# Split expert down pieces: lower halves computed by GpSimd in two operations, upper halves earlier in ScalarE's order, one-hot tables moved

## The reference

```python
def swiglu(x, w_gu, w_dn):
    g, u = jnp.split(x @ w_gu, 2, axis=-1)
    return (jax.nn.silu(g) * u) @ w_dn

for e in range(N_EXPERTS):
    out = out + comb[..., e:e + 1] * swiglu(x, w_gu[e], w_dn[e])
```

## Time and profile before

| what | value |
|---|---|
| median of 3 runs | 1162.55 us (1162.32 to 1163.24) |
| profiled execution, its own time | 1163.06 us |
| profiled execution, span from first to last instruction | 1161.3 us |
| TensorE busy | 1129.7 us, 97% |
| VectorE busy | 928.4 us, 80% |
| ScalarE busy | 686.6 us, 59% |
| GpSimd busy | 26.7 us, 2% |
| mean granted TensorE clock | 0.991 of full speed |
| moved by DMA | 289.34 MB, mean 249 GB/s |

### The profile page before, as it was taken

How to read it: one execution, slowest core, us unless ns; L and a number is a source line. 1 busy time by engine, 2 the same in 40 slices (tenths; PEclk the granted TensorE clock), 3 DMA queues, 4 the chain that set the end, 5 groups by cost and what they waited for, 6 DMA issues and landing times.

```text
span 1161.3 us, 27477 instructions
## 1 busy us (share of the span) xinstructions
PE 1129.7 (97%) x11961; PEld 924.0 (80%) x11961; DVE 928.4 (80%) x1032; ACT 686.6 (59%) x694; POOL 26.7 (2%) x60
## 2 busy tenths in 40 slices
PE   8999999999999999999999998989999999999996
PEld 5888888888888888888888885867777777777574
DVE  6996886789666668896987778979898898989565
ACT  5765744466544446676654447856767667676252
POOL 4000001000000001000001000000000000000000
PEclk9999999999999999999999999989999999999998
DMA  9675565565665664465566655999999999998701
GB/s 290 205 242 189 189 205 196 184 198 164 220 211 183 203 197 136 138 208 192 181 217 222 226 210 190 401 356 406 389 403 384 390 404 384 400 389 336 288 1 39
DMA packets 171070, 289.34 MB, mean 249 GB/s; under 512 B 5195, under 2 KB 132187, under 8 KB 170954
## 3 DMA queue, kind: packets, MB, share of 16 engines
q1 hardware_dynamic: 169040, 283.20, 68.4%
q0 software_dynamic: 1728, 4.16, 1.2%
q10 hardware_dynamic: 202, 0.51, 0.2%
HBM read 286.53 MB, written 1.52 MB: 248 GB/s over the span
## 4 chain that ended last, share of the span: by engine, by line
PE 78%; DVE 16%; ACT 3%; issue 1%; DMA 1%; ACTq 0%; SPq 0%; DVEq 0%
PE acc L599 15%; PE acc L601 15%; PE acc L600 15%; DVE wl L1649 6%; PE aux L950 4%; PE acc L923 3%; PE acc L921 3%; PE acc L922 3%; PE aux L969 2%; ACT wh L1136 2%; PE acc L584 2%; PE acc L591 2%; PE acc L585 2%; DVE side L1655 1%; PE aux L946 1%; PE aux L866 1%
## 5 line engine op out<-in xcount | busy, mean ns | idle before, releaser
L1643 DVE SCALAR_TENSOR_TENSOR wl<-raw,wh 128x2048 f16<-128x2048 f32 x124 | 283.2, 2289 | 85.4 <-ACT wh L1127 84.5
L599 PE MATMUL acc<-xn,wh 128*128 128x264 f16 x1232 | 340.0, 276 | 0.8 <-ACT ya L1179 0.4
L601 PE MATMUL acc<-xn,wl 128*128 128x264 f16 x1232 | 340.0, 276 | 0.0
L600 PE MATMUL acc<-xn,wh 128*128 128x264 f16 x1232 | 340.0, 276 | 0.0
L1127 ACT ACTIVATE wh<-raw 128x2048 f16<-128x2048 f32 x124 | 235.7, 1904 | 1.6 <-DMA raw<-in_w_in 1.6
L922 PE MATMUL acc<-ga,wh 128*128 128x96 f16 x1536 | 199.9, 206 | 0.7 <-issue 0.7
L923 PE MATMUL acc<-ga,wl 128*128 128x96 f16 x1536 | 200.0, 206 | 0.6 <-issue 0.5
L921 PE MATMUL acc<-ga,wh 128*128 128x96 f16 x1536 | 200.0, 206 | 0.0
L1136 ACT ACTIVATE wh<-raw 128x2048 f16<-128x2048 f32 x64 | 122.0, 1911 | 79.9 <-PE acc L923 76.3
L1649 DVE SCALAR_TENSOR_TENSOR wl<-raw,wh 128x2048 f16<-128x2048 f32 x64 | 144.2, 2287 | 17.2 <-ACT wh L1136 17.2
L922 PEld LDWEIGHTS acc<-ga,wh 128*128 128x128 f16 x1536 | 150.5, 98 | 5.0 <-issue 3.3
(11 more groups left out here) (344 smaller groups left out, 1862.6 us busy)
## 6 DMA issues: line engine op xcount, KB each, us to landing
raw<-in_moe_w_gu SPq DMA_DIRECT2D x64, 1024.0 KB, 9.2
raw<-in_w_in SPq DMA_DIRECT2D x56, 1024.0 KB, 5.2
raw<-in_ffn_w_gu SPq DMA_DIRECT2D x24, 1024.0 KB, 5.2
sa<-in_moe_w_gu SPq DMA_DIRECT2D x16, 1024.0 KB, 9.0
xb<-in_moe_w_gu SPq DMA_DIRECT2D x16, 1024.0 KB, 9.3
raw<-in_ffn_w_dn SPq DMA_DIRECT2D x12, 1024.0 KB, 5.1
ya<-in_moe_w_dn SPq DMA_DIRECT2D x10, 1024.0 KB, 9.0
sg<-in_moe_w_dn SPq DMA_DIRECT2D x10, 1024.0 KB, 8.5
```

The source lines that it names most:

```text
L599: nc.tensor.matmul(bank, hi, x[:, 0, x0 + k, :], start=(k == 0), stop=False)
L600: nc.tensor.matmul(bank, hi, x[:, 1, x0 + k, :], start=False, stop=False)
L601: last = nc.tensor.matmul(bank, lo, x[:, 0, x0 + k, :], start=False, stop=(k == k_chunks - 1))
L1643: op(V.scalar_tensor_tensor(out=wl[:, s, 0:size], in0=raw_slot[s][:, 0:size], scalar=WS, in1=wh[:, s, 0:size], op0=ALU.mult, op1=ALU.subtr ...
```

## The change

Four things change. The piece 1 of expert 0 is no longer split, so that 20 split pieces remain. The upper half `hi_dn` of a split piece moves from the end to the front of ScalarE's step, ahead of the two gate/up conversions. The lower half `lo_dn` is taken out of VectorE's stream; GpSimd makes it in two operations instead: it waits for the upper half, multiplies the piece by 256 in its load slot (float32 in place, 128 x 2048), waits for that, and subtracts the upper half from it into the lower one (float16 result). And the one-hot table of an expert is made one expert earlier less two steps: at step 4 of the turn before, in place of step 0.

```diff
--- before.py
+++ after.py
@@ -201,7 +201,7 @@
         def split_down(i):
 
             e, g = i // DN_U, i % DN_U
-            return e < NE - 1 and g in SPLIT_DN
+            return e < NE - 1 and g in SPLIT_DN and i > SPLIT_DN[0]
 
         def splits(i):
 
@@ -237,6 +237,7 @@
         d_loaded = [sem(f"d_loaded{i}") for i in range(D_SLOTS)]
         g_hi, g_lo, gu_mm, dn_mm, y_half = sem("g_hi"), sem("g_lo"), sem("gu_mm"), sem("dn_mm"), sem("y_half")
         dn_hi, dn_lo, hid_h_ready = sem("dn_hi"), sem("dn_lo"), sem("hid_h_ready")
+        dn_scaled = sem("dn_scaled")
         tanh_done, gate_free, hid_e_ready = sem("tanh_done"), sem("gate_free"), sem("hid_e_ready")
         fill_full = [sem(f"fill_full{i}") for i in range(2)]
         fill_done = [sem(f"fill_done{i}") for i in range(2)]
@@ -515,6 +516,13 @@
 
             pool.wait_ge(ga_ready, 4 * LAYERS)
             nc.gpsimd.memset(nt[:, :, 2, :], 0.0).then_inc(nt_clear, 1)
+            for i in range((NE - 1) * DN_U):
+                if split_down(i):
+                    w, k = d_slot[i % D_SLOTS], splits(i) + 1
+                    pool.wait_ge(dn_hi, k)
+                    nc.gpsimd.tensor_scalar(w, w, WS, None, ALU.mult).then_inc(dn_scaled, 1)
+                    pool.wait_ge(dn_scaled, k)
+                    nc.gpsimd.tensor_tensor(dn_h[:, 1, :], w, dn_h[:, 0, :], ALU.subtract).then_inc(dn_lo, 1)
             pool.wait_ge(dn_mm, (NE - 1) * DN_U)
             project_weights(LAYERS - 1)
             pool.wait_ge(aux_done, AX_POS)
@@ -1533,6 +1541,8 @@
             by_token(0)
             for e in range(-1, NE):
                 for g in range(DN_U):
+                    if e >= 0 and split_down(e * DN_U + g + 1):
+                        hi_dn(e * DN_U + g + 1)
                     if e + 2 < NE and g == 3:
                         gathered(e + 2, 2)
                         gathered(e + 2, 3)
@@ -1549,8 +1559,6 @@
                         gathered(e + 2, 1)
                     if e + 2 < NE and g == 3:
                         by_token(e + 2)
-                    if e >= 0 and split_down(e * DN_U + g + 1):
-                        hi_dn(e * DN_U + g + 1)
                     if e == NE - 1 and g in (2, 3, 4):
                         hi(N_PLE[1] + g - 2)
                 if e >= 0:
@@ -1649,12 +1657,6 @@
                 op(V.scalar_tensor_tensor(out=wl[:, j % SLOTS, :], in0=g_slot[j % G_SLOTS], scalar=WS,
                                           in1=wh[:, j % SLOTS, :], op0=ALU.mult, op1=ALU.subtract), g_lo)
 
-            def lo_dn(i):
-
-                vec_e.wait_ge(dn_hi, splits(i) + 1)
-                op(V.scalar_tensor_tensor(out=dn_h[:, 1, :], in0=d_slot[i % D_SLOTS], scalar=WS, in1=dn_h[:, 0, :],
-                                          op0=ALU.mult, op1=ALU.subtract), dn_lo)
-
             def evacuated(n, it=None, step=0):
                 n += 1
                 vec_e.wait_ge(evac_done, n if it is None else it * step + n)
@@ -2290,8 +2292,8 @@
             for e in range(-1, NE):
                 for g in range(DN_U):
                     first = (e + 1) * GU_U + 2 * g + SLOTS
-                    if g == 0 and 2 <= e + 2 < NE:
-                        one_hot(e + 2)
+                    if g == 4 and e + 3 < NE:
+                        one_hot(e + 3)
                     if g == 3 and e + 2 < NE:
                         slot_weights(e + 2)
                     if first < GU_ALL:
@@ -2314,8 +2316,6 @@
                     if e >= 1 and g < 2:
                         add_scattered(e - 1, 4 * g + 2)
                         add_scattered(e - 1, 4 * g + 3)
-                    if e >= 0 and split_down(e * DN_U + g + 1):
-                        lo_dn(e * DN_U + g + 1)
                     if e == NE - 1 and g in (2, 3, 4):
                         lo(N_PLE[1] + g - 2)
                 if e >= 0:
```

## The result

The changed kernel takes 1242.47 us (median of 4 runs, 1242.16 to 1243.49); the kernel before, on the same chip, 1162.43 us (4 runs, 1162.24 to 1163.24). The ratio is 1.0688 [1.0672, 1.0704]: 80 us slower. The prediction said 1180, and 1212 was its upper end. The profiled execution took 1243.49 us, with a span of 1241.8.

What follows compares the result with a forecast made beforehand. TensorE, busy almost the whole span, bounds the kernel; VectorE has only 5.3 us left per expert. Reads held in turn add 21.6 us, expert 0 gains 4.1: 1163.06 becomes 1180.6, stated as 1180 us, range 1153 to 1212.

Steps and rivals of the forecast that it cites:

- GpSimd's reading passes hold VectorE: Expert stage: GpSimd's and VectorE's SBUF reads are served one instruction at a time; the forecast case, 1180 us, chance 0.50.
- Side by side: Rival in the expert stage: GpSimd's reads hold nobody, VectorE has 6.9 us freed per expert; 1155.3 us, chance 0.25.
- GpSimd itself late: Rival in the expert stage: 13.8 us jobs miss the dates when TensorE takes the pieces; 1211 us, chance 0.15.
- the unsplit piece: Piece 1 of expert 0: TensorE takes 3.6 us instead of 8.2, a gain of 4.6 us.
- The upper halves at the front: ScalarE's steps 0, 2 and 4: cost 0, covered by its 13.9 us of waits; bare, 0.6 us per expert.
- the sum: VectorE's time per repeated expert: 35.9 + 18.9 − 3.6 + 1.2 = 52.4 us, 4.3 more than before.
- the price of GpSimd's first pass: GpSimd's one-input pass over 2048 elements, priced from MEMSET and CAST rows at 1.9 us of a 6.3 us job.
- The second: GpSimd's two-input pass over 2048 elements, taken as 4.4 us of a 6.3 us job.
- 3.6 us of overlap: Per expert: half of the 7.1 us of VectorE's PSUM-input operations assumed to run under GpSimd's passes.
- 1.2 us of VectorE idle: Part of VectorE's 5.3 idle us per expert left unusable, since operations sometimes find their conversion not ready.
- below that VectorE still fits: Rival, held but short: with jobs below 4.9 us only expert 0's gain remains; 1158 us, chance 0.10.
- 4.9 us a job: Job length at which the price was to turn: (48.1 − 35.9 + 2.4) / 3, three jobs per expert.

Runs made afterwards that it cites:

- e3: Changed kernel with GpSimd only subtracting (4.1 us jobs, no multiplication; split without the factor 256), all 20 pieces: 1187.99 us.
- e2: Changed kernel with GpSimd's two passes replaced by five memsets of the lower half, about as long but only writing: 1161.64 us.
- e1_rest: Changed kernel with the lower halves back on VectorE at their old place, the other three parts kept: 1155.44 us.
- e4: Kernel before with nine extra GpSimd passes over 128 x 2048 at its start, one after the other, to read their lengths: 1176.78 us.
- e6: Changed kernel with a copy in place instead of GpSimd's multiplication (6.0 us jobs, split without the factor 256): 1200.9 us.
- e5: Changed kernel with both float16 halves of split pieces' hidden values made from one SBUF and one PSUM input each: 1205.01 us.
- e13: e3 with GpSimd subtracting for piece 1 of each expert only; VectorE makes the lower halves of pieces 3 and 5: 1187.11 us.
- e7: e3 with GpSimd subtracting for pieces 3 and 5 only; VectorE makes piece 1's lower half at its old place: 1155.95 us.
- e14: Changed kernel with GpSimd copying and subtracting, unscaled (6.0 us jobs), for pieces 3 and 5 only; VectorE does piece 1: 1163.37 us.
- e11: e3 with the expert's output ahead of the hidden values in VectorE's order: 1178.44 us.
- e8: Changed kernel with its two GpSimd passes for pieces 3 and 5 only; VectorE does piece 1 at its old place: 1195.65 us.
- e12: Changed kernel with the expert's output ahead of the hidden values in VectorE's order: 1235.13 us.

## Why the prediction was wrong

*What held.* That GpSimd's reading passes hold VectorE, and VectorE GpSimd. A subtraction holds a two-input operation to its end (0.36 to 4.19 us in e3), a multiplication only in part (2.29 to 3.34 us), and a multiplication itself goes from 5.36 to 9.34 us; writing alone leaves two-input operations alone (e2, 2286 ns). By the Trainium skill ("SBUF — State Buffer", Who interferes with whom), a VectorE instruction with two SBUF inputs contends with a GpSimd one that reads and not with one that only writes: the trace agrees, with these numbers. Side by side (1155) would have left L2276 at 0.36 us. GpSimd itself late (1211) is refuted: TensorE waited 1.5 us for it, once. Expert 0: 4.6 us predicted for the unsplit piece, 5.2 measured. The upper halves at the front cost nothing that can be seen (e1_rest has TensorE full). The moved one-hot tables and upper halves together gained 3.5 us, where the sum gave them nothing and charged 0.5.

*The step that failed:* the price of GpSimd's first pass, a term of the sum that was too small. The prediction took 1.9 us from the MEMSET and the CAST, 4.6 as its extreme; it is 5.36 to 5.42 (e4). The second was right, 4.4 predicted, 4.05 to 4.57 measured. The job is 9.45 us instead of 6.3, and three of them per expert make the sum 35.9 + 28.4 − 3.6 + 1.2 = 61.9 us, where the trace has 61.7 to 63.3. With it the recorded sum gives 5 × 13.8 = 69.0 for five experts and 38.6 − 6.9 + 28.4 − 2.4 − 48.1 = 9.6 for the last: 1162.6 + 69.0 + 9.6 − 4.1 = 1237, 5 below the measured time (the first expert left at 0; charged like the last it would add 1.3). e6 measures the step without the sum: with 6.0 us jobs the time is 1200.9, inside the predicted range, so 42 of the 62 us by which 1242.5 exceeds the forecast come with the longer first pass. The other 20 are the second fault, below. Nothing in the trace before showed a multiplication on GpSimd, and the bound from a CAST did not contain it.

*Luck in the sum.* That 61.9 meets the trace is in part chance. The prediction took 3.6 us of overlap from no row; VectorE is busy 57.7 us there, so 35.9 + 28.4 − 57.7 = 6.6 us overlapped. And it left 1.2 us of VectorE idle, where the trace has 61.66 − 57.70 = 4.0. The two errors nearly cancel. For e5, which has the same jobs, the same sum is 30 us too high.

*A second fault that this result alone would have hidden:* the sum counted VectorE's time over a whole expert and gave short jobs for free ("below that VectorE still fits"). That is refuted by e3 and e13. The table has the excess over the sum, and the time that TensorE waited at the scattering matmuls for the output or the additions (e1_rest: 0.7 us):

| kernel | jobs, us each | by the sum | measured | over the sum | TensorE's waits |
|---|---|---|---|---|---|
| e7 | 14 x 4.1, pieces 3, 5 | 1155.4 | 1156.0 | 0.5 | 0.7 |
| e14 | 14 x 6.0, pieces 3, 5 | 1155.4 | 1163.4 | 8 | 8.1 |
| e11 | 20 x 4.1, output first | 1155.4 | 1178.4 | 23 | 18.6 |
| e13 | 6 x 4.1, piece 1 | 1155.4 | 1187.1 | 32 | 22.4 |
| e3 | 20 x 4.1 | 1155.4 | 1188.0 | 33 | 22.4 |
| e8 | 14 x 9.45, pieces 3, 5 | 1194 | 1195.7 | 2 | 24.8 |
| e6 | 20 x 6.0 | 1175.5 | 1200.9 | 25 | 37.8 |
| e5 | 20 x 9.45, hidden values from PSUM | about 1235 | 1205.0 | −30 | 38.8 |
| e12 | 20 x 9.45, output first | 1237 | 1235.1 | −2 | 57.2 |
| changed | 20 x 9.45 | 1237 | 1242.5 | 5 | 73.6 |

(Where a job fits by the sum, e1_rest's time stands.) The times follow the waits, in the same order, and not the sum. The job for piece 1 starts just as VectorE comes to the hidden values and the output of an expert, and TensorE then waits for that output. With 4.1 us jobs this place is nearly the whole loss. What piece 5's job holds comes some 20 us earlier, and reaches the output only as far as VectorE doesn't make it good: it no longer makes piece 5's lower half (2.29 us), and in e1_rest it was idle 0.86 us behind that (VectorE's timeline), 3.15 in all:

```profile
842.03 4.49 DVE L1650 SCALAR_TENSOR_TENSOR wl<-raw,wh 128x2048 f16<-128x2048 f32 x2 [0.86 <-ACT wh L1137]
```

An estimate from VectorE's timelines, for one pause, made after the runs and not tried on a new one: what piece 5's job adds to the small operations, less 3.15 and not below 0, plus what piece 1's job adds. e7: 3.1 − 3.15, so 0 (measured 0.4 in all). e14: 4.8 − 3.15 = 1.6 (1.3). e13: 3.8 (3.6). e8: 8.3 − 3.15 = 5.1 (4.0). Changed: 5.1 + 8.4 = 13.5 (12.4). By this estimate held time and place are one account: what counts is the time held between VectorE's last idle moment and the handover. The price turns not at 4.9 us a job but, at piece 1, below 4.1, and at pieces 3 and 5 between 4.1 and 6.0.

Most of the loss is TensorE's idle time. From e1_rest to the changed kernel the span grows by 88.4 us; TensorE is busy 12.6 us longer, for the same matmuls at a lower mean granted clock (0.961 instead of 0.992), and idle 75.8 us longer. The float32 piece behind a pause, 3.64 us before, takes 4.67, 4.89 and 6.26 us behind three of the changed kernel's pauses, and 5.16 in e13.

*Left open.* Why a multiplication holds a two-input operation for only a part of its length, no run shows. A later start of piece 1's job, to pass the hidden values, wasn't tried.

Of the versions run, e1_rest (1155.44 us) beats both kernels; e7 (1155.95) equals it and has GpSimd work for no gain, as TensorE is full in both.

## What to carry to other kernels

Before work goes to GpSimd, look for what VectorE reads from SBUF meanwhile, and ask of each job not only whether its time fits but which operation it will catch, and whether VectorE has an idle moment between that one and its next handover: a 0.36 us operation ahead of a handover to TensorE, held for a pass of 4.1 us, cost 3.6 us of waiting and 1.5 us at the lower clock after it. A price taken from another operation of the same shape (a cast for a multiplication) is no bound; measure that operation alone first, at the kernel's idle start, where nine forms cost one run. And take a change apart: three of the four parts here gained 6.8 us, which the fourth buried.

## What the runs showed of the hardware beyond that

- On GpSimd a multiplication of 128 x 2048 by a constant takes 5.4 us, a copy or cast 1.9 to 2.1, a subtraction of two tensors 4.1 to 4.6, a memset 1.8.
- Memsets, which only write, did hold VectorE's one-input operations from SBUF to SBUF (0.26 us became 0.94 and 1.59 on average). The Trainium skill ("SBUF — State Buffer", Who interferes with whom) has this too: a VectorE tensor_scalar can enter a mode that takes both ports, and then contends with GpSimd; no run shows in which mode it was here. GpSimd's reading passes held these operations too (0.26 us became 4.84 beside a multiplication, and 3.37 beside e7's subtraction). The prediction weighed writing only beside a two-input operation and did not count these.
- A waiting GpSimd pass isn't always served next. The one that was issued at 861.84 took 9.34 us, as long as if it had waited through the end of VectorE's operation in progress and the whole of the next one, to 865.9, when VectorE turned to an operation with a PSUM input. In e5 the one that was issued at 857.09 took only 6.33 us, as if it had started when the operation in progress ended, at 858.1, ahead of the two-input operation behind that. What decides this, no run shows.
